# Four-layer transformer stack on one core: joined order of layer 0's attention, two of its output weights in plain products, and the scale row's multiplication on VectorE

## What is computed

```
mod = silu(c) @ ada_w[l] + ada_b[l]      # 6 rows of 1024: shift, scale, gate (mix), shift, scale, gate (ffn)
h = rms_norm(x, g_pre_mix[l]) * (1 + scale_m) + shift_m
q, k, v, u = split(h @ w_in[l] + b_in[l])           # 8 heads of 64, 2 key/value heads, pool width 512
attn_out = sliding_window_attention_with_sinks(rotary(q), rotary(k), v, sinks[l])   # window 128
pool_out = causal_pool_mixer(u, pool_w[l], pool_scale[l])  # windows 2, 4, 8, 16
mix = concat([attn_out, pool_out]) @ w_out[l]
x = x + gate_m * rms_norm(mix, g_post_mix[l])
h = rms_norm(x, g_pre_ffn[l]) * (1 + scale_f) + shift_f
x = x + gate_f * rms_norm((silu(h @ w_gate[l]) * (h @ w_up[l])) @ w_down[l], g_post_ffn[l])
```

## Time and profile before

| what | value |
|---|---|
| median of 3 runs | 1220.75 us (1219.1 to 1221.16) |
| profiled execution, its own time | 1221.02 us |
| its span, first to last instruction | 1218.9 us |
| mean granted TensorE clock | 0.989 |
| TensorE / VectorE / ScalarE / GpSimd busy | 94% / 67% / 52% / 4% |
| DMA | 252.97 MB, mean 208 GB/s |

### The profile page before, as it was taken

How to read it: one execution, slowest core, us unless ns; L and a number is a source line. 1 busy time by engine, 2 the same in 40 slices (tenths; PEclk the granted TensorE clock), 3 DMA queues, 4 the chain that set the end, 5 groups by cost and what they waited for, 6 DMA issues and landing times.

```text
span 1218.9 us, 19716 instructions
## 1 busy us (share of the span) xinstructions
PE 1150.8 (94%) x7931; PEld 1037.4 (85%) x7931; DVE 822.1 (67%) x1273; ACT 634.9 (52%) x1106; POOL 43.8 (4%) x73
## 2 busy tenths in 40 slices
PE   5859999999989899999999999999999999999998
PEld 3447899999777799999898789999989878999996
DVE  5798867798793865555658477656665857766563
ACT  3155633454644744344656676545455567654553
POOL 2200000000200100010000000000000000000000
PEclk9989899999999999999999999999999999999999
DMA  9968599999461476567244256555535424655530
GB/s 379 408 231 345 209 259 303 299 393 349 155 261 36 162 272 236 212 179 291 93 172 173 74 190 219 203 177 203 176 108 182 156 87 175 206 204 178 199 113 34
DMA packets 37305, 252.97 MB, mean 208 GB/s; under 512 B 4416, under 2 KB 4704, under 8 KB 8928
## 3 DMA queue, kind: packets, MB, share of 16 engines
q1 hardware_dynamic: 34992, 244.47, 56.4%
q0 software_dynamic: 2080, 7.25, 1.8%
...
q10 hardware_dynamic: 144, 0.00, 0.0%
...
## 4 chain that ended last, share of the span: by engine, by line
PE 81%; DVE 10%; DMA 3%; ACT 3%; issue 1%; SPq 0%; DVEq 0%; ACTq 0%
PE bank L479 25%; PE bank L481 25%; PE bank L480 25%; DMA raw_w<-weights 3%; PE bank L486 3%; DVE raw_w L1485 3%; DVE lo_w L1475 2%; PE bank L528 2%; ACT gtok L1097 1%; DVE prob L1612 1%; DVE smax L1615 1%; PE bank L874 1%; DVE normed L1558 1%; DVE prob L1621 1%; PE bank L594 0%
## 5 line engine op out<-in xcount | busy, mean ns | idle before, releaser
L1475 DVE TENSOR_TENSOR lo_w<-raw_w,hi_w 128x1024 fp32r<-128x1024 f32 (+2 forms) x354 | 418.9, 1209 | 135.6 <-ACT hi_w L1092 135.5
L1092 ACT ACTIVATE hi_w<-raw_w 128x1024 fp32r<-128x1024 f32 (+2 forms) x354 | 358.0, 1040 | 182.4 <-DMA raw_w<-weights 117.3
L479 PE MATMUL bank<-in_hi,lo_w 128*128 128x256 f32 x1408 | 395.6, 281 | 0.0
L480 PE MATMUL bank<-in_lo,hi_w 128*128 128x256 f32 x1408 | 392.8, 279 | 0.0
L481 PE MATMUL bank<-in_hi,hi_w 128*128 128x256 f32 x1408 | 392.7, 279 | 0.0
L479 PEld LDWEIGHTS bank<-in_hi,lo_w 128*128 128x128 f32 x1408 | 264.3, 188 | 2.6 <-issue 0.8
L480 PEld LDWEIGHTS bank<-in_lo,hi_w 128*128 128x128 f32 x1408 | 263.6, 187 | 1.9 <-issue 0.5
L481 PEld LDWEIGHTS bank<-in_hi,hi_w 128*128 128x128 f32 x1408 | 264.7, 188 | 0.0
L479 PE MATMUL bank<-hi_w,in_lo 128*128 128x256 f32 (+2 forms) x496 | 157.3, 317 | 11.8 <-DVE in_lo L1574 5.2
L480 PE MATMUL bank<-lo_w,in_hi 128*128 128x256 f32 (+2 forms) x496 | 154.3, 311 | 0.0
L481 PE MATMUL bank<-hi_w,in_hi 128*128 128x256 f32 (+2 forms) x496 | 154.3, 311 | 0.0
(11 more groups left out here) (208 smaller groups left out, 1068.4 us busy)
## 6 DMA issues: line engine op xcount, KB each, us to landing
...
```

The costliest lines, as they stand in the source:

```text
L479: nc.tensor.matmul(o, st[1], mv[0], start=start, stop=False, **kw)
L480: nc.tensor.matmul(o, st[0], mv[1], start=False, stop=False, **kw)
L1092: nc.scalar.activation(hi_w[:, m % NSPLIT, cut], raw_view(unit)[:, cut], ACT.Identity).then_inc(*sig("hi_w", unit, i))
L1475: nc.vector.tensor_tensor(lo_w[:, m % NSPLIT, cut], raw_view(unit)[:, cut], hi_w[:, m % NSPLIT, cut].bitcast(F32), ALU.subtract).then_inc( ...
```

## The change

- The units of ada in layer 0 are placed anew: 8, 9, 10, 11, 16, 17, 18 first, then wo(0,0), 19, wo(0,1), 12, 13, 14, 15. VectorE's and ScalarE's orders in layer 0's attention are rewritten to it. ada 14 and 15 go into the boundary, as do the splits of gu(0,0) and gu(0,1); those of gu(0,2) and gu(0,3) follow behind it.
- wo(0,2) and wo(0,3) leave the stream. They are loaded whole into free memory behind ada(0,9) and ada(0,10), and `whole_into_y` makes plain f32 products of them with `raw`, between the transposes of the probabilities. ScalarE scales the pooled tiles into `raw` (`pool_whole`).
- In layer 0 ScalarE multiplies the probabilities by the inverted sum (`shares`), in 16 pieces; VectorE only inverts. In layer 1 ScalarE rounds the scaled pooled tiles straight from PSUM (`pool_hi`) and VectorE takes the remainder from PSUM (`pool_lo`); the products with wo(1,2) and wo(1,3) stand between the transposes of the probabilities; ada(1,15) stands behind wo(1,3).
- The middle constants (masks and pool bands) are loaded ahead of ada(0,9) instead of ahead of wo(0,2).
- `scale` moves from GpSimd's order to VectorE's, in all three boundaries that have it; on VectorE it stands directly ahead of `norm`. Where it is taken out of GpSimd's order, the DMAs around it stay.

The diff, cut to its core and with less indentation (left out: the list of parameters, the input and the place of the whole weights, a renamed buffer, GpSimd's `scale` and its three calls, which are removed; where "..." stands inside the orders of ScalarE and VectorE, lines of before, are taken out):

```diff
@@ -121,13 +121,12 @@
 ADA_AFTER = {
-    ("wo", 0, 2): [(0, 10)], ("wo", 0, 3): [(0, 11), (0, 16), (0, 17)],
-    ("wo", 0, 0): [(0, 18), (0, 19), (0, 12)], ("wo", 0, 1): [(0, 13), (0, 14), (0, 15)],
+    ("wo", 0, 0): [(0, 19)], ("wo", 0, 1): [(0, 12), (0, 13), (0, 14), (0, 15)],
 }
 _order = [(0, 20 + _i) for _i in range(4)] + [(1, _i) for _i in range(12)] + [(1, 16 + _i) for _i in range(4)]
 _f = [("gu", 0, _i) for _i in range(2, 22)]
 ADA_AFTER.update({_u: [_a] for _u, _a in zip(_f, _order)})
-ADA_AFTER.update({("in", 1, 2): [(1, 12)], ("in", 1, 3): [(1, 13)], ("in", 1, 4): [(1, 14)], ("wo", 1, 2): [(1, 15)]})
+ADA_AFTER.update({("in", 1, 2): [(1, 12)], ("in", 1, 3): [(1, 13)], ("in", 1, 4): [(1, 14)], ("wo", 1, 3): [(1, 15)]})
 ADA_AFTER.update({("gu", 1, 4 + 4 * _i): [(1, 20 + _i)] for _i in range(4)})
@@ -160,7 +159,7 @@
             units.append((("ada", 0, n), *SHAPES["ada"]))
-    for n in (8, 9):
+    for n in (8, 9, 10, 11, 16, 17, 18):
         units.append((("ada", 0, n), *SHAPES["ada"]))
@@ -170,7 +169,8 @@
                 add(kind, L, i)
-        for i in (2, 3, 0, 1) if L < 2 else (0, 1, 3, 2):
+        for i in ((0, 1), (2, 3, 0, 1), (0, 1, 3, 2), (0, 1, 3, 2))[L]:
             add("wo", L, i)
...
              ("ada", 0, 3): (6, 7)}
+WHOLE_AFTER = {("ada", 0, 9): 2, ("ada", 0, 10): 3}
...
         done.then_inc(*sig("used", unit))
+def whole_into_y(u, T):
+    pe.wait_ge(*due(f"whole_in{u}"))
+    for c in range(2):
+        job = ("y", 0, 0, T, c)
+        if u == 2:
+            take(job, 2 * T + c)
+        for n in range(2):
+            t = 2 * u + n
+            pe.wait_ge(*due("pool_cat", 0, t // 2 - 2))
+            done = nc.tensor.matmul(ps(job)[:, :], half(raw[:, t, :], T), whole[u][:, n, cols(c)], start=(u == 2 and n == 0), stop=False)
+    if T == 1:
+        done.then_inc(*sig("used_whole", u))
...
             slice_of(7, T, c).then_inc(*sig("in", 0, T, c))
-        banks(7, 0, 3, 4, 5, 6, 1, 2)
+        banks(4, 5, 6, 7, 2, 3)
         scores_late()
     else:
-        banks(4, 5, 6, 7, 0, 1, 2, 3, 4, 5, 6, 7, 2, 3, 0, 1)
+        banks(4, 5, 6, 7, 0, 1, 2, 3, 4, 5, 6, 7, 2, 3)
         both_halves(lambda T: ("in", 1, T, 1), ("in", 1, 2))
...
-    turn_prob(0)
-    turn_prob(1)
+    banks(0, 1, *((4, 6, 5, 7) * 4))
     pe.wait_ge(*due("const_mid", 0))
...
         last.then_inc(*sig(*job))
-    for n in range(3, 6):
+    for n, (T, u) in enumerate(((0, 2), (0, 3), (1, 2), (1, 3)), 1):
         turn_prob(n)
+        if L == 0:
+            whole_into_y(u, T)
+        else:
+            into_y(1, 0, ("wo", 1, u), T, first=(u == 2))
+    turn_prob(5)
...
-    banks(4, 5, 6, 7)
-    for q, u in enumerate((2, 3)):
-        for T in range(2):
-            into_y(L, 0, ("wo", L, u), T, first=(q == 0))
-        attention(q)
+    for jp in range(2):
+        attention(jp)
     spread_row(L, "gate", 0)
...
         sp.dma_start(vrow[:, :], a_vec).then_inc(*sig("vec_in", 0, by=16))
-    if unit == ("wo", 0, 2):
+    if unit == ("ada", 0, 9):
         sp.dma_start(const[:, const_mid:const_late], a_const[:, const_mid:const_late]).then_inc(*sig("const_mid", 0, by=16))
...
     off += P * kt * n_cols
+    if unit in WHOLE_AFTER:
+        u = WHOLE_AFTER[unit]
+        sp.dma_start(whole[u].rearrange("p t c -> p (t c)"), a_whole[u - 2, :, :]).then_inc(*sig(f"whole_in{u}", by=16))
     for kk in INK_AFTER.get(unit, ()):
...
     sc.wait_ge(*due(f"raw_w{UNIT_NO[unit] % NRAW}", unit))
-    if m < 3:
-        sc.wait_ge(*due("ink_used", (1, 3, 3)[m]))
+    if m < 2:
+        sc.wait_ge(*due("ink_used", (1, 3)[m]))
+    elif m < NSPLIT:
+        sc.wait_ge(*due("used_whole", 2))
     if m >= NSPLIT:
...
         row_in(0, "scale", 1)
+        x_root(0)
+        y_squares(1, 0)
+        y_squares(1, 1)
+        y_root(1)
+        prepare(("gu", 0, 0))
+        row_in(0, "shift", 1)
+        prepare(("gu", 0, 1), (0,))
+        x_root(1)
+        rounded(0, 0)
+        rounded(0, 1)
+        prepare(("gu", 0, 1), (1,))
+        rounded(1, 0)
+        rounded(1, 1)
+        for unit in units:
+            prepare(unit)
+        return
     x_root(0)
     if not units:
         x_root(1)
         return
     prepare(units[0], (0,))
     y_squares(1, 0)
...
+    rounded(0, 0)
+    rounded(0, 1)
+    y_squares(1, 1)
     y_root(1)
...
...
+    def exps(n):
+        nh, w = (2, 257) if n < 4 else (4, 129)
+        sc.wait_ge(*due("smax", L, n))
+        for i in range(nh):
+            last = nc.scalar.activation(prob[:, n, w * i:w * i + w], prob[:, n, w * i:w * i + w], ACT.Exp,
+                                        bias=smax[:, n, i:i + 1], scale=-1.0, accum_out=ssum[:, n, i:i + 1])
+        last.then_inc(*sig("exp", L, n))
+    def shares(n):
+        nh, w = (2, 257) if n < 4 else (4, 129)
+        sc.wait_ge(*due("over_sum", L, n))
+        for i in range(nh):
+            p_ = prob[:, n, w * i:w * i + w - 1]
+            last = nc.scalar.activation(p_, p_, ACT.Identity, scale=ssum[:, n, i:i + 1])
+        last.then_inc(*sig("prob", L, n))
+    def pooled_in():
+        for i in range(2):
+            copy(("pool", L, i), pooled[:, 2 * i:2 * i + 2, :].rearrange("p t s -> p (t s)"), ps(("pool", L, i))[:, :], "pooled", L, i)
+    def pool_whole():
+        for i in range(2):
+            sc.wait_ge(*due("poolw", 0, i))
+            for g in range(2):
+                t = 4 + 2 * i + g
+                last = nc.scalar.activation(raw[:, t, :], ps(("poolw", 0, i))[:, 256 * g:256 * (g + 1)], ACT.Identity,
+                                            scale=v("pool_scale0", 2 * i + g))
+            last.then_inc(*sig("pool_cat", 0, i, frees=("poolw", 0, i)))
+    def pool_hi():
+        for i in range(2):
+            sc.wait_ge(*due("poolw", L, i))
+            for g in range(2):
+                t = 4 + 2 * i + g
+                last = nc.scalar.activation(in_hi[:, t, :], ps(("poolw", L, i))[:, 256 * g:256 * (g + 1)], ACT.Identity,
+                                            scale=v(f"pool_scale{L}", 2 * i + g))
+            last.then_inc(*sig("pool_hi", L, i))
+    if L == 0:
+        qk_in(0, 0)
+        qk_in(1, 0)
+        qk_in(0, 1)
+        qk_in(1, 1)
+        exps(0)
+        pooled_in()
+        exps(1)
+        shares(0)
+        exps(2)
+        shares(1)
+        pool_whole()
+        exps(3)
+        shares(2)
+        probT_in(0)
+        exps(4)
+        shares(3)
+        probT_in(1)
+        exps(5)
+        shares(4)
+        probT_in(2)
+        shares(5)
+        probT_in(3)
+    else:
         prepare(("in", 1, 4))
         for T in range(2):
             qk_in(T, 0)
         prepare(("wo", 1, 2))
         for T in range(2):
             qk_in(T, 1)
+        for n in range(4):
+            exps(n)
         prepare(("wo", 1, 3))
...
+        pooled_in()
+        exps(4)
+        probT_in(0)
+        exps(5)
+        pool_hi()
+        for n in range(1, 4):
+            probT_in(n)
+    prepare(("wo", L, 0))
+    for n in range(4, 6):
         probT_in(n)
...
     prepare(("wo", L, 1))
...
         row_in(L, "shift", 1)
-    prepare(("gu", L, 0))
-    prepare(("gu", L, 1))
+        prepare(("gu", 1, 0))
+        prepare(("gu", 1, 1))
...
         in_turn(unit)
-    if m < 3:
+    if m < 2:
         ve.wait_ge(*(due("ink_used", 5) if m == 0 else due("in", 0, 1, 2)))
+    elif m < NSPLIT:
+        ve.wait_ge(*due("used_whole", 3))
     for i in parts:
...
                 *sig("x", *job[1:], frees=job))
+def scale(N, T):
+    for c in range(2):
+        if T == 0:
+            ve.wait_ge(*(due("row1", N[1], "scale", 0) if N[0] == "mix" else due("row", N[1], "scale", 1, c)))
+        else:
+            ve.wait_ge(*due("normed", N, 0, c))
+        ve.wait_ge(*due("x", *before(N), T, c))
+        nc.vector.tensor_tensor(scaled[:, cols(c)], x[:, T, cols(c)], rows[:, 1, cols(c)], ALU.mult).then_inc(*sig("scaled", N, T, c))
...
     residual(L, w, 0)
+    if (L, w) == (0, 0):
+        ada(0, 14)
+        gain(0, 0, 1, 0)
+        gain(0, 0, 1, 1)
+        ada(0, 15)
+        residual(0, 0, 1)
+        scale(N, 0)
+        norm(N, 0)
+        lo(("gu", 0, 0))
+        rest(0, 0)
+        rest(0, 1)
+        scale(N, 1)
+        norm(N, 1)
+        lo(("gu", 0, 1))
+        rest(1, 0)
+        rest(1, 1)
+        for unit in units:
+            lo(unit)
+            behind(unit)
+        return
+    if modulated(N):
+        scale(N, 0)
     norm(N, 0)
...
     residual(L, w, 1)
+    if modulated(N):
+        scale(N, 1)
     norm(N, 1)
...
...
+    def scored(n):
+        if n < 4:
+            softmax(L, n, 2, 256, 257, 0.125, k("window"), prob, 6)
+        else:
+            softmax(L, n, 4, 128, 129, 0.125, k("causal2", P, 2 * P), prob, 6)
+    def over_sum(n):
+        nh = 2 if n < 4 else 4
+        ve.wait_ge(*due("exp", L, n))
+        nc.vector.reciprocal(ssum[:, n, 0:nh], ssum[:, n, 0:nh]).then_inc(*sig("over_sum", L, n))
+    def shares(n):
```

(65 more changed lines are left out.)

120 lines of the change are left out of this document (13 added, 107 removed).

## The result

The changed kernel takes **1205.68 us** (median of 4 runs, 1204.89 to 1208.41) against 1220.81 (4 runs) in the same session: ratio 0.9883 [0.9864, 0.9901]. The forecast was 1207.0, range 1199 to 1215. The profiled execution took 1206.20 (span 1204.3, clock 0.991), 14.8 us less than the one of before.

A forecast was written before the change was run, and what follows sets the result against it. TensorE (94% busy) bounds the kernel, VectorE layer 0's attention. Layer 0 9.5, scale row 2.0 and layer 1's attention 2.5 sum to 14.0 us off 1221.02: 1207.0, range 1199 to 1215.

The forecast's parts named there:

- (a): Layer 0's attention: ScalarE no longer rounds wo(0,2) ahead of the q/k copies; first score pass 60.59 to 57.9, 2.7 us.
- (b): Layer 0's attention: VectorE's work from first score pass to boundary falls from 54.8 to 34 us.
- (c): Layer 0's attention: ScalarE's multiplications cost 5.7 us, VectorE waits 3.6 and 0.9, reaching the boundary near 96.5 us.
- (d): Layer 0's attention: 16 plain TensorE products at 0.43 us take 6.9 us for 11.7, in VectorE's shadow.
- dear plain products: Rival, layer 0's attention: plain products cost 0.98 us each, last turn and attention slip 3 us; 1210 us, chance 0.03.
- The boundary: Behind layer 0's attention: TensorE idles, spreads maybe at lower clock; costs 8 of 19 us won, front ends 130 to 131.5.
- Feed-forward 0: Layer 0's feed-forward, behind the front products: as long as before (170 us), change 0.
- starving rival: Layer 0's feed-forward: weight splits come late, three holes lose 7 us each, 1228 us; chance 0.06.
- The scale row: Boundaries (0,1) and (1,0): scale multiplications on VectorE end the norm earlier, 1.0 us each, minus 2.0 together.
- Layer 1's attention: Layer 1: scores start earlier, first into_y at 366.2 for 371.84; minus 2.5 us, bounds 0 and minus 6.
- The sum: Whole kernel: 9.5 + 2.0 + 2.5 = 14.0 us off the profiled 1221.02, giving 1207.0; chance 0.57.
- The signs: Wrong if: plain products 0.9 apart, VectorE awaiting raw_w's DMA over 3 us, TensorE idle 135-300, first front product after 120.

The follow-up runs named there:

- the move of ada(0,15): Against the changed kernel, ada(0,15) prepared on VectorE right behind ada(0,14), ahead of the second tokens' gains: 1201.34 us, ratio to before 0.9839.

## Why the prediction was right, step by step

- **(a), (b), (c)** hold: first score pass 57.58 (57.9), first gain 95.65 (near 96.5), the wait for wo(0,0) 3.60 (3.6). ScalarE's shares of 256 and 128 columns took 0.90 us for two and 1.26 for four, 0.40 and 0.29 from start to start (0.41 and 0.30 taken).
- **(d) was mis-sized by half**: 0.43 us was taken for a plain product, 0.90 was measured. The step that failed was dividing the input product's 30 us by the matmul rows: each product of this kind has two. The 16 take 14.4 us, not 6.9, and more than the 11.7 of the three-pass product that they replace. The result stood because the other half of the sentence held, that they lie in the shadow of another engine; only this is ScalarE (shares, copies, wo(0,0)) and not VectorE. This shadow was about as long as the products are: half of them left out bring the attention forward by 1.0 us, all of them twice put it back by 14.5. That it was long enough for twice the price was luck, since the forecast put only 6.9 us into it. The rival "dear plain products" had the price right (0.98 taken, 0.90 measured) and the consequence wrong: it has the last turn and the attention slip by 3 us. The last turn did end late, at 83.60, where the forecast has the products done at 81 and where it ended at 81.85 with half of them left out; the attention could have come only 1.0 us sooner, since ScalarE's copies were not ready. The four-pass rule of the Trainium skill's FP8 and Floating Point Precision (TensorE Precision Notes) counts four passes, which makes an estimate of 0.98 us from the single pass of 0.244 us; the trace, with 0.90, agrees within a tenth.
- **The boundary** came as worked out, with its price: idle 4.41 us, spreads at half clock. That this wasn't necessary is what the move of ada(0,15) shows.
- **Feed-forward 0** was taken at 0 and lost 1.4 us (0.5 to 1.4 by the eight traces). It is the starving rival in small. Its price of 7 us a hole was far off: three waits of 0.3, 0.2 and 0.4 us.
- **The scale row**: -1.0 at each later boundary, as forecast.
- **Layer 1's attention** gave 4.1 us for 2.5. The first into_y came 6.1 us earlier against its boundary, for 5.6 worked out. The 1.6 us too many are half clock in the first 24 products of before's one execution, which the other execution of the same order didn't have; against that one (77.04) after gains 2.6, as forecast.
- **The sum** of 14.0 stands against 14.5 in the table and 14.8 in the profiled executions' own times. Minus 0.3 in layer 0, plus 1.4 in feed-forward 0 and minus 1.6 in layer 1 nearly cancel; so that the total came within 0.8 us is in part luck.
- **The signs**: one of those of being wrong came, the plain products 0.9 us apart. Of the others, the first front product came at 115.71 (not later than 120), and TensorE's waits in feed-forward 0 add up to 0.9 us.
- **Left open**: whether the three-pass products of the pooled half (11.7 us for 14.4) would have done as well between the turns, with the same new order; no run tried it. By the price alone they would be the cheaper on TensorE, but they need the splits on ScalarE and VectorE.
